# Hybrid GLA, S5 and RG-LRU layer on one core: GLA's first six projection bands computed before the LRU stage ends, with weight buffers shared by three stages

## The reference, cut to what matters

```
h = x * (1 + scale1) + shift1
q, k, v, r, glr, u, lx, ly, gates = split(h @ w_in)
logits = glr @ gla_w_gate + gla_b_gate
log_a = log_sigmoid(logits) / 16
xc = centred_depthwise_conv(lx)
a = exp(-8 * softplus(-lam) * sigmoid(xc @ w_a + b_a))
b = sqrt(1 - a * a) * sigmoid(xc @ w_i + b_i) * xc
y_lru = (scan_forward(a, b) + scan_backward(a, b)) * gelu(ly)
```

## Time and profile before

| | |
|---|---|
| median of three runs | 3084.89 us (3084.51 to 3085.87) |
| the profiled execution, device time | 3078.54 us |
| its span in the profile | 3076.8 us |
| mean granted TensorE clock | 0.969 |
| busy: PE, DVE, ACT, POOL | 94%, 59%, 38%, 26% |

### The profile page before, as it was taken

The page is one execution under the profiler, slowest core; times in us unless marked ns, Lnnn a source line. Parts: engine busy times, 40 slices in busy tenths (PEclk is TensorE's granted clock), DMA queues, the critical chain, the costliest instruction groups (busy, mean ns, idle before and its releaser), DMA issues. The chain is left out here.

```text
span 3076.8 us, 41867 instructions
## 1 busy us (share of the span) xinstructions
PE 2885.9 (94%) x17008; PEld 2788.7 (91%) x17008; DVE 1804.7 (59%) x2382; ACT 1162.2 (38%) x1759; POOL 802.9 (26%) x381
## 2 busy tenths in 40 slices
PE   6999976999999789899996999999999999999996
PEld 6999976878988689899996999999999999999996
DVE  7788872234343489999995454788762332233226
ACT  2789892334343432344444110112572112211224
POOL 0233311101100024555532333334211221111223
PEclk9999997999999789999998999999999999999998
DMA  5112102001110035434445354635111111111111
GB/s 219 53 50 75 50 34 64 30 22 33 38 34 24 33 110 192 137 118 118 119 113 177 110 199 149 200 126 189 42 42 42 42 44 46 42 42 42 42 42 69
DMA packets 111180, 257.82 MB, mean 84 GB/s; under 512 B 20960, under 2 KB 54752, under 8 KB 110752
## 3 DMA queue, kind: packets, MB, share of 16 engines
q1 hardware_dynamic: 100928, 214.26, 21.8%
q10 hardware_dynamic: 10080, 41.18, 3.6%
HBM read 199.01 MB, written 56.37 MB: 83 GB/s over the span
## 5 line engine op out<-in xcount | busy, mean ns | idle before, releaser
L2605 PE MATMUL bank<-yhi,mrg_hi 128*128 128x384 f32 x1560 | 525.2, 337 | 3.8 <-POOL mrg_lo L2535 2.1
L2605 PE MATMUL bank<-yhi,mrg_lo 128*128 128x384 f32 x1560 | 521.8, 334 | 0.0
L2605 PE MATMUL bank<-ylo,mrg_hi 128*128 128x384 f32 x1560 | 521.8, 334 | 0.0
L2535 POOL TENSOR_TENSOR mrg_lo<-mrg_raw,mrg_hi 128x1024 fp32r<-128x1024 f32 x69 | 169.3, 2454 | 678.6 <-ACT mrg_hi L2713 678.5
L2572 PE MATMUL bank<-yhi,mrg_hi 128*128 128x384 f32 x864 | 291.0, 337 | 28.0 <-POOL mrg_lo L167 22.8
L2605 PEld LDWEIGHTS bank<-yhi,mrg_hi 128*128 128x128 f32 x1560 | 293.3, 188 | 7.7 <-POOL mrg_lo L2535 3.0
L2605 PEld LDWEIGHTS bank<-ylo,mrg_hi 128*128 128x128 f32 x1560 | 293.4, 188 | 1.1
L2605 PEld LDWEIGHTS bank<-yhi,mrg_lo 128*128 128x128 f32 x1560 | 293.3, 188 | 0.0
L2572 PE MATMUL bank<-yhi,mrg_lo 128*128 128x384 f32 x864 | 289.8, 335 | 0.0
L2572 PE MATMUL bank<-ylo,mrg_hi 128*128 128x384 f32 x864 | 289.8, 335 | 0.0
L1739 PE MATMUL bank<-hhi,s_hi 128*128 128x384 f32 x768 | 265.6, 346 | 19.5 <-POOL s_lo L180 19.5
(11 more groups left out here) (406 smaller groups left out, 6538.1 us busy)
## 6 DMA issues: line engine op xcount, KB each, us to landing
mrg_raw<-in_mlp_units SPq DMA_DIRECT2D x64, 512.0 KB, 3.6
s_raw<-in_s_units SPq DMA_DIRECT2D x32, 512.0 KB, 4.5
mrg_scr<-in_w_ada_rows SPq DMA_DIRECT2D x32, 512.0 KB, 3.6
mid_gates<-gate ACTq DMA_DIRECT2D x24, 576.0 KB, 3.1
gt<-mid_gates SPq DMA_DIRECT2D x24, 576.0 KB, 3.8
gla_raw<-in_gla_units SPq DMA_DIRECT2D x25, 512.0 KB, 3.7
lru_raw<-in_lru_units SPq DMA_DIRECT2D x24, 512.0 KB, 3.9
x<-in_x_t SPq DMA_DIRECT2D x16, 576.0 KB, 9.8
```

The source lines that it names most:

```text
L2535: pool.tensor_tensor(WLO[SLOT[u]], S.raw[u % 2], WHI[SLOT[u]].bitcast(F32), ALU.subtract).then_inc(S.split_done, 1)
L2605: mm = pe.matmul(out, wt[SLOT[u]][:, w], r[:, k, band_cols(b)], start=(k == first and y == 0), stop=(k == last and y == 2))
```

## The change

Three things are changed.

1. The weight buffers become the property of `Core`: `weight_buffers(hctx)` allocates them once, beneath the LRU, GLA and S5 stages, and a second set is allocated for the merge. So a weight tile can outlive its stage.
2. At the close of the LRU stage, SP loads GLA's units 0 to 3 behind the last LRU units (as units 24 to 27 of the LRU's stream). ACT and POOL split units 0 and 1 in blocks 10 and 11 and unit 2 after the end of ACT's work. PE makes six bands (units 0 and 1, glr and q) behind its last gate products, in PSUM banks 0, 1, 5, 6, 7 and 2, and they stay there. The second of the two waits in the loop is for all gates to be emptied, the third for ly's banks. In the last block, `evac_y` (with a table change on either side) moves from the middle of ACT's sigmoids to behind its square roots. SP ends the stage only when the six bands are made and three units are split.
3. The GLA stage starts with its semaphores counted up as if these units were done. ACT empties the six bands first; PE starts with band 6 (the first of k), then the three gate products, then bands 7 to 11. SP's first transfers are the small tables; the first weight load there is unit 4.

```
 UW = 1024
 PROJ0 = 7
+AHEAD = 2
+AHEAD_BANK = (0, 1, 5, 6, 7, 2)
...
+    def weight_buffers(self, ctx):
+        self.raw, self.hi, self.lo = ([ctx.enter_context(self.nc.sbuf_tensor(f"w{self.stage}_{part}{s}", [P, UW], dt)) for s in range(2)]
+                                      for part, dt in (("raw", F32), ("hi", F32R), ("lo", F32R)))
...
+        NEXT = 2 * LBLK
...
+                def source(u):
+                    return dram["lru_units"][u] if u < NEXT else dram["gla_units"][u - NEXT]
+
                 def load_x(i):
-                    if i < LBLK:
-                        S.load(sync, 2 * i, 0, dram["lru_units"][2 * i])
+                    if i < LBLK + 2:
+                        S.load(sync, 2 * i, 0, source(2 * i))
...
                 sync.wait_ge(y_out, 16 * LBLK)
+                sync.wait_ge(S.raw_in[1], 16 * (LBLK + 2))
+                sync.wait_ge(S.split_done, 2 + NEXT + 3)
+                sync.wait_ge(gla_mm, AHEAD * NB)
...
                 for i in range(LBLK):
-                    if i + 1 < LBLK:
-                        S.split_lo(pool, 2 * i + 3, 1)
-                    if i + 2 < LBLK:
-                        S.split_lo(pool, 2 * i + 4, 0)
+                    S.split_lo(pool, 2 * i + 3, 1)
+                    S.split_lo(pool, 2 * i + 4, 0)
...
+                pe.wait_ge(x_free, NB * LBLK)
+                for n in range(AHEAD * NB):
+                    if n == 2:
+                        pe.wait_ge(g_free, GN * LBLK)
+                    if n == AHEAD * NB - 1:
+                        pe.wait_ge(y_free, NB * LBLK)
+                    band(NEXT + n // NB, n % NB, core.bank[AHEAD_BANK[n]][:, 0:BW]).then_inc(gla_mm, 1)
...
                 def unit_hi(u):
-                    if u < 2 * LBLK:
-                        if u >= 2:
+                    if u == NEXT + 2:
+                        act.wait_ge(gla_mm, NB)
+                    if u <= NEXT + 2:
+                        if 2 <= u < NEXT + 2:
...
-                        if b == 1 and i:
+                        if b == 1 and 0 < i < LBLK - 1:
                             evac_y(i)
                             act.activation(warm[:], tiny[:], ACT.Sigmoid)
-                    unit_hi(2 * i + 4)
+                    if i + 1 < LBLK:
+                        unit_hi(2 * i + 4)
...
+                evac_y(LBLK - 1)
+                unit_hi(NEXT + 2)
...
+        def band_bank(n):
+            return core.bank[AHEAD_BANK[n] if n < AHEAD * NB else n % 2][:, 0:BW]
...
-                sync.sem_inc(S.split_done, 2)
+                sync.sem_inc(S.split_done, 2 + AHEAD + 1)
+                sync.sem_inc(S.hi_done, AHEAD + 1)
+                for par in range(2):
+                    sync.sem_inc(S.raw_in[par], 32)
+                sync.sem_inc(band_mm, AHEAD * NB)
...
-                    if n >= 2:
-                        pe.wait_ge(band_free, n - 1)
-                    out = core.bank[n % 2][:, 0:BW]
+                    pe.wait_ge(band_free, n - 1 if n >= AHEAD * NB + 2 else n - AHEAD * NB + 1)
+                    out = band_bank(n)
...
+                band(AHEAD * NB)
                 pe.wait_ge(const_done, 6)
-                for n in range(NB):
-                    band(n)
-                pe.wait_ge(band_free, NB)
+                pe.wait_ge(band_free, AHEAD * NB)
                 pe.wait_ge(small_in, 64)
                 for key in PRE_GATES:
                     item(key)
-                for n in range(NB, 4 * NB):
+                for n in range(AHEAD * NB + 1, 4 * NB):
                     band(n)
...
-                unit_hi(0)
-                unit_hi(1)
+                for n in range(AHEAD * NB):
+                    evac_band(n)
                 act.wait_ge(const_done, 6)
                 act.wait_ge(small_in, 64)
-                for n in range(NB):
-                    evac_band(n)
                 for key in PRE_GATES:
                     evac_item(key)
+                evac_band(AHEAD * NB)
                 log_gates(0, 0)
```

More of the change, by code:

```diff
@@ L122, with __init__ @@
 class Stream:
-    def __init__(self, core, ctx, name, raw_width=UW):
-        nc = core.nc
+    def __init__(self, core, name):
         self.core = core
-        self.memory = ctx.enter_context(nc.sbuf_tensor(f"{name}_raw", [P, 2 * raw_width], F32))
-        self.raw = [self.memory[:, s * raw_width:s * raw_width + UW] for s in range(2)]
-        self.hi = [ctx.enter_context(nc.sbuf_tensor(f"{name}_hi{s}", [P, UW], F32R)) for s in range(2)]
-        self.lo = [ctx.enter_context(nc.sbuf_tensor(f"{name}_lo{s}", [P, UW], F32R)) for s in range(2)]
+        self.raw, self.hi, self.lo = [r[:] for r in core.raw], core.hi, core.lo
         self.raw_in = [core.sem(f"{name}_raw_in{s}") for s in range(2)]
@@ L220, in modulate_and_lru @@
         NSR, NSC = 4, 5
-        S = Stream(core, ctx, "lru")
+        S = Stream(core, "lru")
         lw_raw = sb("lw_raw", [P, 4 * P])
@@ L277, in _ @@
                 sync.sem_inc(S.split_done, 2)
+                def source(u):
+                    return dram["lru_units"][u] if u < NEXT else dram["gla_units"][u - NEXT]
                 def load_x(i):
-                    if i < LBLK:
-                        S.load(sync, 2 * i, 0, dram["lru_units"][2 * i])
+                    if i < LBLK + 2:
+                        S.load(sync, 2 * i, 0, source(2 * i))
                 def load_y(i):
-                    if i < LBLK:
-                        S.load(sync, 2 * i + 1, 1, dram["lru_units"][2 * i + 1])
+                    if i < LBLK + 2:
+                        S.load(sync, 2 * i + 1, 1, source(2 * i + 1))
                 def load_gates(i):
@@ L709, in sem @@
             return core.sem(name)
-        S = Stream(core, ctx, "gla")
+        S = Stream(core, "gla")
         glr = sb("glr", [P, T])
@@ L884, in store_y @@
                     sync.dma_start(dram["y_gla"][2 * h + 2 + w][:, cols], o[h % 2][:, w, cols]).then_inc(y_out[b], 16)
-                load(0)
                 sync.dma_start(wgate[0:64], dram["gla_wgate"]).then_inc(small_in, 16)
                 sync.dma_start(params[:], dram["gla_params"]).then_inc(small_in, 16)
-                load(1)
                 sync.dma_start(keep[:], dram["keep"]).then_inc(small_in, 16)
@@ L892, in _ @@
                 load_cached(0)
-                for u in range(2, 7):
+                for u in range(4, 7):
                     load(u)
@@ L930, in _ @@
                         pool.memset(probs[d][s][:], 0.0).then_inc(const_done, 1)
-                for u in range(len(UNITS)):
+                for u in range(AHEAD + 1, len(UNITS)):
                     S.split_lo(pool, u, u % 2)
@@ L1057, in unit_hi @@
                 def unit_hi(u):
-                    if u < len(UNITS):
-                        if u >= 2:
-                            act.wait_ge(band_mm, NB * (u - 1))
+                    if AHEAD < u < len(UNITS):
+                        act.wait_ge(band_mm, NB * (u - 1))
                         S.split_hi(act, u, u % 2, u // 2, None)
@@ L1066, in evac_band @@
                     cols = slice(b * BW, (b + 1) * BW)
-                    src = core.bank[n % 2][:, 0:BW]
+                    src = band_bank(n)
                     act.wait_ge(band_mm, n + 1)
@@ L1147, in square @@
                     act.activation(osq[(NB * h + b) % 2][:], o[h % 2][:, :, y * BW:(y + 1) * BW], ACT.Square).then_inc(sq_done, 1)
-                unit_hi(0)
-                unit_hi(1)
+                for n in range(AHEAD * NB):
+                    evac_band(n)
                 act.wait_ge(const_done, 6)
                 act.wait_ge(small_in, 64)
-                for n in range(NB):
-                    evac_band(n)
                 for key in PRE_GATES:
                     evac_item(key)
+                evac_band(AHEAD * NB)
                 log_gates(0, 0)
-                for n in range(NB, 3 * NB):
+                for n in range(AHEAD * NB + 1, 3 * NB):
                     evac_band(n)
@@ L1434, in s5_and_gates @@
         RESET = (NCC, NCS)
-        S = Stream(core, ctx, "s5")
+        S = Stream(core, "s5")
         pww = [sb(f"pww{c}", [P, GROUPS, SCH]) for c in "ri"]
@@ L2249, in merge_and_mlp @@
         UNIT = [0, 8, 24, 32, 40]
-        S = Stream(core, ctx, "mrg")
+        S = Stream(core, "mrg")
         yhi = sb("yhi", [P, LBLK, T], F32R)
@@ L3101, in build @@
             hlo = hctx.enter_context(nc.sbuf_tensor("hlo", [P, KD, T], F32R))
+            core.weight_buffers(hctx)
             modulate_and_lru(core, hhi, hlo, mod)
@@ L3105, in build @@
         x1 = ctx.enter_context(nc.sbuf_tensor("x1", [P, KD, T], F32))
+        core.weight_buffers(ctx)
         merge_and_mlp(core, mod, x1)
```

1 line of the change is left out of this document (added).

## The result

| | before | after |
|---|---|---|
| median of timed executions, us | 3084.7 (4; 3077.89 to 3085.87) | 3044.61 (4; 3042.18 to 3046.9) |
| profiled execution, us | 3078.54 | 3046.9 |
| its span, us | 3076.8 | 3045.1 |
| granted clock, mean | 0.969 | 0.975 |

The change is faster: ratio 0.9875, 95% interval 0.9861 to 0.989, or some 40 us between the medians. From profiled execution to profiled execution the gain is 31.6 us, and 31.2 were forecast. The document has to explain both: why the steps hold, and where the other 8.5 us between the medians come from.

The account below looks back on a forecast made before the run. PE, busy 94%, was taken as the bound, its 35.0 us wait before GLA as the time to win. Opening gain 33.6 less seam 2.4 is 31.2 us; off the median 3084.9 that gives 3053.7, range 3048.5 to 3060.5.

Parts of the forecast that it names:

- PE's longest wait bounds the opening, and a band ahead is worth its PE time: GLA's opening, seam to key transposes: without the 35.0 us wait and six bands, 65.4 us become 31.8, gain 33.6.
- The covers that got thinner: GLA's opening: the gates-to-keys chain, some 19 us, fits beside five bands (21.8); emptying bands 7 and 8 costs nothing, bound 1.
- Block 10's y at 450.7, ACT's tables right then: LRU's last blocks: a split meeting DVE delays block 10's y to near 450.7, so ACT's exponentials start as before.
- The gelu's move buys nothing at the end: LRU block 11: the 3.9 us taken out of ACT's sigmoids buy nothing but room for PE.
- The tail pays one split, 2.3: LRU's tail: unit 26's split meets DVE's multiplication and lengthens the tail by 2.3 us, bounds 0 and 2.34.
- The rival that it is not lengthened: LRU's tail not lengthened, PE sets the seam at about 475.8: gain 34.8, time 3050.1 us; chance 23%.
- The seam 2.4 later: End of the LRU stage: POOL's first GLA instruction moves from 477.0 to 479.4, costing 2.4 us.
- PE is done before DVE: Beneath the LRU's tail: PE's six bands end at 474 to 475, before DVE's last y at 475.2.
- the rival in which PE ends the LRU stage: LRU's end: bands at 1.2 GHz make PE set the seam, near 484; gain put at 25, 3059.9 us; chance 21%.
- Nothing runs ahead: LRU's tail: a wait holds PE until its end, only the first load's 7.96 less 0.8 saved: 3077.7 us; chance 3%.
- slower by the clock: GLA's dense run not granted full clock, 0.15 us lost a matmul; at 300 matmuls 3098.7 us; chance 3%.
- The difference is taken off that median: 3084.9 - 31.2.: Whole kernel: the 31.2 us gain from the profiled execution, 6.4 below the three-run median, is taken off that median, giving 3053.7.

Follow-up runs that it names:

- e13: The changed kernel run again without an edit: median 3052.11 us (6 executions), ratio 0.9909.
- e12: Changed kernel with the gelu of the last ly back among the sigmoids of block 11: median 3054.04 us, ratio 0.9903.
- e3: Changed kernel with POOL's last split (GLA's unit 2) held until DVE's last y is out: median 3048.24 us, ratio 0.9888.
- e4: Changed kernel with both splits held behind DVE's y (unit 1 behind block 10's, unit 2 behind the last): median 3042.71 us, ratio 0.9878.
- e1: The kernel before, run again without an edit: median 3083.45 us (11 executions); profiled span 3089.2 us.
- e8: Changed kernel with three bands made ahead in place of six: median 3063.82 us, ratio 0.9937.

## Why the prediction was right, and where it was not

- *PE's longest wait bounds the opening, and a band ahead is worth its PE time.* Right. The opening took 30.0 against 31.8 forecast. By terms: 0.9 to PE's start (0.8), band 6 in 5.7 up to the gate products (6.8), those 2.5 (2.4), five bands 20.9 (21.8). The part most off is the low clock in band 6, some 1.4 in place of 2.6. That it was less here is chance and not the shorter rest: after rests of 8 to 9.2 us the four profiles of after lost 1.4, 1.5, 2.3 and 2.9 (24 matmuls against the same at full clock), and after 35 us the kernel before lost 2.7 in its first profile and 1.4 to 1.6 in three others. The forecast's choice of 2.6, with 0 to 3.5 as bounds, was a fair one.
- *The covers that got thinner.* They held: no rest of note stands between band 7 and the keys.
- *Block 10's y at 450.7, ACT's tables right then.* Right to 0.3 us (450.38, 450.45). The detail was wrong: POOL began first, at 442.33, and DVE's scan waited for it, 4.42 us. The forecast had POOL waiting and the addition paying; e13, an execution of the same kernel, shows that order. Which of the two pays changes from execution to execution with who began first (split 442.33 and scan 442.58 in after, scan 440.37 and split 440.53 in e13); the cost was 2.09 us on the scan and 1.4 on the addition.
- *The gelu's move buys nothing at the end.* Right: 0.2 to 0.8 us in e12.
- *The tail pays one split, 2.3.* Right: 2.09 in e3. The rival that it is not lengthened fell. The page "SBUF — State Buffer" of the Trainium skill, section "Who interferes with whom", has the two engines lock each other out whole. The scans agree: 2.33 became 4.42, 0.42 became 2.51, both by 2.09.
- *The seam 2.4 later.* It was 1.95 (478.95 against 479.4) from one profile to the other, and 3.5 in the mean of four each. With the opening's 34.4 the means give 30.9 for the two terms, where 31.2 were forecast.
- *PE is done before DVE.* Right, with more room than forecast: its bands ended at 470.6, not 474 to 475, at a granted clock of 1.00 throughout, and it stood 9.2 us. So the rival in which PE ends the LRU stage fell. Wrong was its companion, that PE would stop a shorter tail at a seam of 475.8: e4's is at 472.4.
- *Nothing runs ahead*, and *slower by the clock*: both fell. The mean granted clock rose from 0.969 to 0.975. The clock did fall in GLA, but in either kernel.
- *The agreement to 0.4 us.* It is in part luck. Between the two profiles the opening gave 1.8 more than forecast and the seam took 0.4 less, but the rest of GLA took 1.9 that the forecast had at nothing.
- *The range's low end.* For an opening with no low clock it takes off 1.6 us, where the sum has 2.6 for it. With 2.6 the end is 3047.5, still above the measured time.
- *"The difference is taken off that median: 3084.9 - 31.2."* This is the step that failed. It takes one execution of before, puts the change on it, and then moves the sum by 6.4 us to the median, as if the distance between an execution and the median were the same in the next kernel. It is not: single executions of either kernel differ by 19 us and more, in after's case in good part by whether a stretch near the end of head 0 is granted 1.2 or 2.4 GHz. The profiled execution of before had no such stretch and lay 6.4 below the median (e1, 6 us above it, had it, and a longer merge besides); the four of after were all of its lower group, which is chance as far as is known. Profile against profile, 3047.3 was forecast and 3046.9 measured; mean against mean, 31.2 and 31.6. And 3053.7 lies between the two groups of after, 1.4 us from the mean of its 21 executions. What failed with the shift is the range: it was made of the bounds of the steps alone and had no term for this scatter, though the steps of head 0 without a band are in the kernel before as well. The 6.4 us alone, taken off its low end, give 3042.1, and the range would have held 3044.61; the 6 to 9 us that the low stretch cost would have done so too.

## What to carry to other kernels

When an engine at 94% has one long rest, move work of its own from behind the rest into it: each piece is worth its whole time. Before taking such work in, ask which other engine sets the rest's end, and keep each preparing split or copy off it: here one wait placed behind DVE's y was worth 2 us, two of them 3.5 to 4. And before a difference is put on a median, look for stretches where the main engine works with gaps, since there the clock may be granted in one execution and not in the next; put that difference into the range, and compare many executions or profiles part by part. When two windows of two executions are compared, count both from the same instruction: 0.6 us of offset is enough to make equal work look unequal.

## What was not expected of the hardware

- The clock fell to 1.2 GHz for 17 to 24 us after PE had only worked with rests of 1.0 to 1.3 us, with no long idle time. In other executions it stayed, though PE had done the same work up to that moment (19.28 and 19.29 busy of 22.70 us). That costs 6 to 9 us in some executions of an unchanged program.
- What a restart loses to the clock did not go by the length of the rest: 1.4 to 2.9 us after 8 to 9.2 us (four executions of after), 1.4 to 2.7 after 35 (four with before's opening), 2.9 after 22.0 (e8).
- A scan with three SBUF inputs is held by a GpSimd split just as an addition is, and a tile of 128 columns pays the same 2.09 us as one of 1024. I read that as the wait for the split's end, not a sharing.
- Moving the buffers of three stages to other addresses changed S5 and the merge by 0.1 us or less.
